# Decode steps of a retention layer moved from TensorE to VectorE and ScalarE

## What is computed

```python
# one step for a sample: chunk length C = 1, per head
S_new = gamma * S + outer(k, v)        # k * k_decay = k, as C - 1 - idx = 0
o     = q @ S_new                      # intra + cross of retention_chunk
```

## Time and profile before

| | |
|---|---|
| median of 3 runs | 1497.14 us |
| profiled execution, first to last instruction | 1495.6 us |
| TensorE clock granted, mean | 0.997 |
| instructions | 28307 |
| bytes moved by DMA | 229.13 MB, mean 153 GB/s |
| VectorE, ScalarE, POOL instructions | 1251, 929, 571 |

### The profile page before, as it was taken

How to read it: one execution, slowest core, us unless ns; L and a number is a source line. 1 busy time by engine, 2 the same in 40 slices (tenths; PEclk the granted TensorE clock), 3 DMA queues, 4 the chain that set the end, 5 groups by cost and what they waited for, 6 DMA issues and landing times.

```text
span 1495.6 us, 28307 instructions
## 1 busy us (share of the span) xinstructions
PE 1475.2 (99%) x11336; PEld 1455.2 (97%) x11336; DVE 1001.0 (67%) x1251; ACT 635.4 (42%) x929; POOL 842.0 (56%) x571
## 2 busy tenths in 40 slices
PE   8999999999999999999999999999999999999996
PEld 5999999999999999999999999999999999999995
DVE  7999888856545724576715876766657765574847
ACT  5533444344544541131213855556556332332333
POOL 3377776777545653257565445555555655554555
PEclk9999999999999999999999999999999999999998
DMA  6013333322356258621421144566759575454634
GB/s 217 22 42 94 114 114 113 113 80 65 112 176 205 75 200 296 219 80 50 149 78 50 29 149 171 199 237 219 253 193 326 203 285 189 142 208 156 227 107 170
DMA packets 110091, 229.13 MB, mean 153 GB/s; under 512 B 8960, under 2 KB 20992, under 8 KB 108304
## 3 DMA queue, kind: packets, MB, share of 16 engines
q1 hardware_dynamic: 95296, 204.30, 39.7%
q10 hardware_dynamic: 14672, 23.09, 4.6%
HBM read 154.41 MB, written 72.95 MB: 152 GB/s over the span
## 4 chain that ended last, share of the span: by engine, by line
PE 96%; POOL 1%; DMA 1%; ACT 1%; issue 1%; DVE 0%; POOLq 0%; SPq 0%; DVEq 0%; ACTq 0%
PE ps L1476 40%; PE ps L1237 26%; PE ps L1026 16%; PE ps L1402 3%; PE ps L1389 3%; PE ps L1074 2%; PE ps L1164 1%; PE ps L1169 1%; PE ps L1180 1%; PE ps L1166 1%; DMA cva_h<-conv_scratch 1%; PE ps L1147 0%; PE ps L1152 0%; PE ps L1194 0%; POOL w_l L931 0%
## 5 line engine op out<-in xcount | busy, mean ns | idle before, releaser
L1476 PE MATMUL ps<-tx_h,w_h 128*128 128x258 f32 x960 | 271.5, 283 | 0.0
L1476 PE MATMUL ps<-tx_l,w_h 128*128 128x258 f32 x960 | 271.3, 283 | 0.0
L1476 PE MATMUL ps<-tx_h,w_l 128*128 128x258 f32 x960 | 271.1, 282 | 0.0
L996 POOL TENSOR_TENSOR w_l<-raw,w_h 128x512 fp32r<-128x512 f32 x120 | 185.6, 1551 | 147.6 <-ACT w_h L2033 147.1
L1476 PE MATMUL ps<-fx_l,w_h 128*128 128x258 f32 x720 | 203.7, 283 | 0.0
L1476 PE MATMUL ps<-fx_h,w_h 128*128 128x258 f32 x720 | 203.6, 283 | 0.0
L1476 PE MATMUL ps<-fx_h,w_l 128*128 128x258 f32 x720 | 203.4, 282 | 0.0
L1476 PEld LDWEIGHTS ps<-tx_h,w_h 128*128 128x128 f32 x960 | 181.4, 189 | 0.1
L1476 PEld LDWEIGHTS ps<-tx_l,w_h 128*128 128x128 f32 x960 | 181.4, 189 | 0.1
L1476 PEld LDWEIGHTS ps<-tx_h,w_l 128*128 128x128 f32 x960 | 181.2, 189 | 0.0
L2328 DVE SCALAR_TENSOR_TENSOR ps<-u_ext,wdw,ps 128x512 f32<-128x512 f32 x232 | 155.2, 749 | 0.0
(11 more groups left out here) (386 smaller groups left out, 4305.4 us busy)
## 6 DMA issues: line engine op xcount, KB each, us to landing
raw<-wseq_dram SPq DMA_DIRECT2D x260, 256.0 KB, 3.1
quad_scratch<-quad_h SPq DMA_DIRECT2D x16, 774.0 KB, 3.5
tx_h<-quad_scratch SPq DMA_DIRECT2D x12, 1032.0 KB, 10.4
tx_l<-hidden_scratch SPq DMA_DIRECT2D x12, 1032.0 KB, 12.8
gate_scratch<-gst SPq DMA_DIRECT2D x10, 1032.0 KB, 5.0
hidden_scratch<-hq_g SPq DMA_DIRECT2D x8, 1032.0 KB, 7.0
hidden_scratch<-stg_b SPq DMA_DIRECT2D x6, 1032.0 KB, 6.9
hq_g<-hidden_scratch SPq DMA_DIRECT2D x6, 1032.0 KB, 13.1
```

Source lines behind the costliest of these rows:

```text
L996: pool.tensor_tensor(lo, src, hi.bitcast(F32), ALU.subtract).then_inc(q_lo, 1)
L1476: out = pe.matmul(ps[:, 2 * n + s, 0:HC], RINGS[q % RING][wa][:, kk * P:(kk + 1) * P], OPS[x][xb][:, QK * kh + kk, at_:at_ + HC], start=(i ...
```

## The change

The state of a sample now lies with the values on partitions: `s_in` and `rets` are laid out by the host as (sample, pair, 128, 512), where the 512 columns are head, half of the values and key dimension. Then o is a sum over columns. VectorE multiplies by broadcast rows of key and query, adds into the decayed state and sums; ScalarE decays the state in place. The rows that are transposed on TensorE and broadcast through memory are keys and queries (2 x 2 x 128) instead of values. `decode_out` and `decode_copy` are gone, and with them their waits. The row buffer `rows_b` is used for the products too, so the next row load waits for `dec_o`, which the last sum raises.

```diff
-DEC_LOAD = {1: 0, 4: 1, 7: 2, 10: 3, 14: 4, 17: 5, 21: 6, 24: 7}
-DEC_STATE = {3: 0, 6: 1, 9: 2, 13: 3, 16: 4, 20: 5, 23: 6, 27: 7}
-DEC_OUT = {4: 0, 9: 1, 11: 2, 14: 3, 18: 4, 21: 5, 25: 6, 30: 7}
-DEC_COPY = {x + 1: n for x, n in DEC_OUT.items()}
+DEC_ROWS = 5
+DEC_LOAD = {7 + 3 * b: b for b in range(DEC)}
+DEC_STATE = {9 + 3 * b: b for b in range(DEC)}
+DEC_STORE = {10 + 3 * b: b for b in range(DEC)}
...
-            def v_decode(p):
-
-                for t in range(4):
-                    out = pe.transpose(ps[0:DEC, 7, t * P:(t + 1) * P], vv[p][:, t, SEQ:T], ident[:])
-                out.then_inc(vs_T, 1)
+            def sample_rows(p):
+
+                for n, t in enumerate((2, 3, 0, 1)):
+                    out = pe.transpose(ps[0:DEC, 7, n * P:(n + 1) * P], qk[p][:, t, SEQ:T], ident[:])
+                out.then_inc(row_T, 1)
...
                 if x in RET_A:
                     if RET_A[x] == 0:
-                        pe.wait_ge(vs_cp, 1)
+                        pe.wait_ge(ln_n, 8)
+                        x_evicted(pe, X_V[0][1], "e5")
+                        x_evicted(pe, X_V[0][1], "e7")
+                        pe.wait_ge(rope_done, 4)
+                    if RET_A[x] == 2:
+                        pe.wait_ge(row_cp, 1)
                     chunk_a(0, RET_A[x])
...
-                if x in DEC_OUT:
-                    n = DEC_OUT[x]
-                    x_evicted(pe, v if j > 1 else v - 1, "e2")
-                    if n:
-                        pe.wait_ge(dec_cp, n)
-                    decode_out(0, n, 2 * decode_bank(x), HC + 2 + 4 * n).then_inc(dec_o, 1)
+                if x == DEC_ROWS:
+                    pe.wait_ge(s_upd, 3)
+                    sample_rows(0)
...
+                last.then_inc(mm, 1)
                 chunk_b(1, c)
-                if c > 1:
-                    last = decode_out(1, c - 2, 3 * (g % 2), CH + 8)
-                last.then_inc(mm, 1)
...
             def decode_load(p, b):
...
+                n = b + DEC * p
+                act.wait_ge(ss_st[b % 2], 16 + 16 * (n // 2))
+                if n > 1:
+                    act.wait_ge(dec_o, n - 1)
+                act.dma_start(s_dec[:, b % 2, :], s_in[b, p]).then_inc(ss_ld[b % 2], 16)
+
+            def row_load(p, b):
+
+                n = b + DEC * p
+                if n:
+                    act.wait_ge(dec_o, n)
+                act.wait_ge(row_st, 16 * p + 16)
+                act.dma_start(rows_b[:], rscr[p, b:b + 1, :].broadcast_to([P, 4 * DK])).then_inc(row_ld, 16)
+
+            def decode_decay(p, b):
+
+                n = b + DEC * p
+                act.wait_ge(ss_ld[b % 2], 16 * (n // 2 + 1))
+                for h in range(2):
+                    s_h = s_dec[:, b % 2, h * DV:(h + 1) * DV]
+                    act.activation(s_h, s_h, ACT.Copy, scale=float(GAMMA[2 * p + h])).then_inc(s_dcy, 1)
...
                 if i == 4:
-                    act.wait_ge(dec_cp, DEC * (p + 1))
+                    act.wait_ge(dec_o, DEC * (p + 1))
...
-                if v == X_GB[3]:
-                    act.wait_ge(s_new, DEC + 1)
...
             for c in range(NRC):
                 chunk_values(1, c)
                 if c > 1:
+                    decode_decay(1, c - 2)
                     decode_store(1, c - 2)
                 if c:
                     decode_load(1, c - 1)
-                    value_load(1, c - 1)
+                    row_load(1, c - 1)
                 chunk_output(1, c)
...
+            decode_decay(1, DEC - 2)
             state_store(1)
             taken(act, G_AOUT + NRC - 1)
             norm_square(1, 0)
             decode_store(1, DEC - 2)
             decode_load(1, DEC - 1)
-            value_load(1, DEC - 1)
+            row_load(1, DEC - 1)
             norm_square(1, 1)
             for i in range(2 * CHUNKS):
                 norm_root(1, i)
                 if i == 0:
+                    decode_decay(1, DEC - 1)
+                if i == 1:
                     decode_store(1, DEC - 1)
...
             def decode_state(p, b):
...
+                n = b + DEC * p
+                s_b = s_dec[:, b % 2, :]
+                dve.wait_ge(s_dcy, 2 * n + 2)
+                dve.wait_ge(row_ld, 16 * n + 16)
+                for t in range(4):
+                    s_t = s_b[:, t * P:(t + 1) * P]
+                    out = dve.scalar_tensor_tensor(s_t, rows_b[:, (t // 2) * DK:(t // 2 + 1) * DK],
+                                                   vv[p][:, t, SEQ + b:SEQ + b + 1], s_t, ALU.mult, ALU.add)
                 out.then_inc(s_new, 1)
...
+                dve.wait_ge(s_new, n + 2)
+                q = rows_b[:, 2 * DK:].rearrange("p (h d) -> p h d", h=2)
+                for e in range(2):
+                    out = dve.tensor_tensor(rows_b[:, 2 * e * DK:2 * (e + 1) * DK].rearrange("p (h d) -> p h d", h=2),
+                                            s_b.rearrange("p (h e d) -> p e h d", h=2, e=2)[:, e], q, ALU.mult)
+                out.then_inc(dec_pr, 1)
+                dve.wait_ge(dec_pr, n + 1)
+                for e in range(2):
+                    out = dve.reduce_sum(vv[p].rearrange("p (h e) n -> p e h n", e=2)[:, e, :, SEQ + b],
+                                         rows_b[:, 2 * e * DK:2 * (e + 1) * DK].rearrange("p (h d) -> p h d", h=2),
+                                         mybir.AxisListType.X)
+                out.then_inc(dec_o, 1)
```

More of the change, by code:

```diff
@@ L342, in build @@
         ss_st = [sem("ss_st0"), sem("ss_st1")]
-        vb_ld = sem("vb_ld")
-        s_kv = sem("s_kv")
+        row_ld = sem("row_ld")
+        s_dcy = sem("s_dcy")
         s_new = sem("s_new")
@@ L1172, in chunk_b @@
                 out.then_inc(ret_b, 1)
[L1174 to L1183, removed]
             def out_stat(p, i):
@@ L1213, in unit_bank @@
                     x_evicted(pe, v - 1, "e2")
-                    read = [n for x, n in DEC_OUT.items() if x <= turn(v, 1)]
-                    if read:
-                        pe.wait_ge(dec_cp, max(read) + 1)
                 elif k == 4:
@@ L1330, in b_part @@
                         between(sub)
-                if g in (G_BO0, G_BO0 + 1):
-                    out = decode_out(1, DEC - 2 + g - G_BO0, 3 * (g % 2), CH + 8)
                 out.then_inc(mm, 1)
@@ L1656, in sig_rows, with sample_rows_out @@
                 act.activation(sgm[:, k:k + n, :] if v in X_G else rows, rows, ACT.Sigmoid).then_inc(xg_sg, 1)
-            def v_decode_out(p):
-                act.wait_ge(vs_T, p + 1)
-                act.activation(v_bc[0:DEC], ps[0:DEC, 7, :], ACT.Copy).then_inc(vs_cp, 1)
-                act.wait_ge(vs_cp, p + 1)
-                act.dma_start(vscr[p], v_bc[0:DEC]).then_inc(vs_st, 16)
+            def sample_rows_out(p):
+                act.wait_ge(row_T, p + 1)
+                act.activation(rows_b[0:DEC], ps[0:DEC, 7, :], ACT.Copy).then_inc(row_cp, 1)
+                act.wait_ge(row_cp, p + 1)
+                act.dma_start(rscr[p], rows_b[0:DEC]).then_inc(row_st, 16)
             def ln_square(j):
@@ L1711, in decode_load @@
             def decode_load(p, b):
-                act.wait_ge(ss_st[b % 2], 16 + 16 * (b // 2 + p * (DEC // 2)))
-                if p == 0 and b > 1:
-                    act.wait_ge(dec_o, b - 1)
-                elif p == 1 and b < 2:
-                    act.wait_ge(dec_o, DEC)
-                elif p == 1:
-                    act.wait_ge(mm, done(S_AOUT + b))
-                act.dma_start(s_dec[:, b % 2, :].rearrange("p (h e) -> p h e", h=2),
-                              s_in[b, 2 * p:2 * p + 2].rearrange("h p e -> p h e")).then_inc(ss_ld[b % 2], 16)
-            def value_load(p, b):
-                act.wait_ge(s_new, b + NRC * p + 1)
-                act.wait_ge(vs_st, 16 * p + 16)
-                act.dma_start(v_bc[:], vscr[p, b:b + 1, :].broadcast_to([P, 2 * DV])).then_inc(vb_ld, 16)
+                n = b + DEC * p
[15 more added lines that the diff above has]
+                    act.activation(s_h, s_h, ACT.Copy, scale=float(GAMMA[2 * p + h])).then_inc(s_dcy, 1)
             def decode_store(p, b):
-                act.wait_ge(s_new, b + NRC * p + 2)
-                act.dma_start(rets[b, 2 * p:2 * p + 2].rearrange("h p e -> p h e"),
-                              s_dec[:, b % 2, :].rearrange("p (h e) -> p h e", h=2)).then_inc(ss_st[b % 2], 16)
+                act.wait_ge(s_new, b + DEC * p + 2)
+                act.dma_start(rets[b, p], s_dec[:, b % 2, :]).then_inc(ss_st[b % 2], 16)
             def state_store(p):
@@ L2491, in decode_state @@
-                dve.wait_ge(s_kv, n * 2 + 2)
-                for h in range(2):
-                    hs = slice(h * DV, (h + 1) * DV)
-                    out = dve.scalar_tensor_tensor(s_dec[:, b % 2, hs], s_dec[:, b % 2, hs], float(GAMMA[2 * p + h]),
-                                                   v_bc[:, hs], ALU.mult, ALU.add)
-                out.then_inc(s_new, 1)
-            def decode_copy(p, b, bank, col):
```

(3 more changed lines are left out.)

66 lines of the change are left out of this document (20 added, 46 removed).

## The result

The changed kernel takes 1499.49 us (median of 20 runs, 1498.21 to 1500.97), the kernel before in the same comparison 1497.38: a ratio of 1.0014, interval 1.0008 to 1.0020. The forecast was 1485.7. The profiled execution has a span of 1497.8 us where the one before had 1495.6.

What follows compares the result with a forecast made beforehand. TensorE, busy 99%, was taken as the bound: -14.4 us of decode matmuls, +1.2 in pair 0, +1.8 in the tail, -11.4 in sum, giving 1485.7 us. The range was 1482.6 to 1490.5, holding some 0.83.

Steps and rivals of the forecast that it cites:

- What leaves TensorE: Decode matmuls in both pairs: 0.90 us per step, 16 steps, 14.4 us removed, all on the path.
- What ScalarE gets: Two decays per step, 0.7 us, 11 us in all; POOL's ring slot freed sooner in pair 1 priced at nothing.
- The new wait: Row load waits for dec_o; in the A_OUT loop a worst row delays a step 2 us, inside over 3 us slack.
- Rival (d): A_OUT loop paced by the single row buffer's round trip, making the kernel slower: 1501.7 us; chance 0.05.
- The ports: VectorE stretched beside POOL's work: one stretch of 1.0 us per step, chance 6 in 8 in pair 0, none in loop.
- six of the eight sets: Pair 0 sets counted as having a VectorE stretch beside POOL before the change; basis for the 6 in 8 odds.
- Pair 0, the tight places: Steps 1, 3, 5 make TensorE wait 0.9, 0.6, 0.1 us if stretched; 1.2 us with odds, bounds 0 and 4.6.
- The tail: End of pair 1: round trip step 6, row, step 7 gives back 1.8 of 2.7 us, bounds 0.9 and 2.9.
- VectorE's undisturbed step: A decode step on VectorE without hold-ups: 2.5 us, one more than before, 16 us over the kernel.

Runs made afterwards that it cites:

- x2: Changed kernel with each decode step's two-input VectorE operations (state update, query product) replaced by reductions of the same widths: 1483.31 us, ratio 0.9902 to the kernel before.
- x16: Changed kernel with semaphore mm rising in chunk_b again in pair 1's A_OUT loop, so GpSimd's split starts later: 1491.44 us, ratio 0.9959 to the kernel before.
- x7: Changed kernel with pair 0's steps at other turns, state loads ahead of stores, and steps of four 512-column VectorE instructions: 1494.90 us, ratio 0.9980 to the kernel before.
- x13: x7 plus GpSimd waiting in the A_OUT loop for the chunk's decode step before splitting the next weight slot: 1488.69 us, ratio 0.9938 to the kernel before.

## Why the prediction was wrong

**What leaves TensorE: right.** The period of a chunk is 9.43 us as forecast (584.75 to 594.18 in the chain of waits), and x2 is 14.2 us below the kernel before, against 14.4.

**What ScalarE gets: the step that failed.** "POOL's ring slot is freed a few us sooner in pair 1 [...]: nothing, since POOL waits for the ring and not PE for it" looked at who waits for POOL, and not at what POOL's work runs beside. The freed slot started the split 3.4 us earlier in the chunk, next to VectorE's new step. x16 puts the semaphore back to where the split begins 5.2 us after chunk_a instead of 3.0: 8.0 us. In the terms of the sum, pair 1 gave back 8.0 us where 1.8 were charged, and pair 0 gave back 8.2 (5.7 of waits and 2.5 of half clock) where 1.2 were. The first is this step, the second the size of the port stretches with what followed from it, below.

**The new wait: half right.** The late row came as forecast (8.50 us, step 4 late by 1.9), inside TensorE's slack. But the slack was read for TensorE alone; 2 us late was enough to fall beside GpSimd, which kept steps 5 and 6 late in their turn. Rival (d), a round trip that paces the loop, is not what happened: the period stayed at 9.43.

**The ports: mis-sized, in the loop from nothing.** Charged were 1.0 us per stretch in pair 0 and none in the loop, because before there was none in the loop. But before, GpSimd stood elsewhere in the chunk. The count of "six of the eight sets" was misread too. Only two of the six stretches lay in the fused operations. The others lay in the copy and in the multiply by a scalar, which have one SBUF input and which the new step does not have, such as these two of the trace of before:

```profile
390.43 1.67 DVE L2489 TENSOR_SCALAR v_bc<-v_bc,qk 128x256 f32<-128x256 f32 x2
...
490.31 1.25 DVE L2484 COPY qd_b<-qk 128x2 f32<-128x2 f32 x1
```

And a block is not held once: each of several operations in a row can be held by a GpSimd instruction of its own. The four of step 4 in pair 0 took 3.98 us where 1.14 is free, and those of step 5 3.83. Of the four of step 4 one took 341 ns and the others 1116 to 1381, beside three GpSimd instructions:

```profile
469.84 3.98 DVE L2470 SCALAR_TENSOR_TENSOR s_dec<-rows_b,v,s_dec 128x128 f32<-128x128 f32 x4 [1.63 <-ACT s_dec L1706]
...
479.83 3.83 DVE L2470 SCALAR_TENSOR_TENSOR s_dec<-rows_b,v,s_dec 128x128 f32<-128x128 f32 x4 [0.31 <-ACT s_dec L1706]
...
469.52 1.29 POOL L930 TENSOR_TENSOR wx_l<-wx_y,wx_h 128x512 fp32r<-128x512 f32 x1
470.95 1.41 POOL L912 TENSOR_TENSOR wx_y<-raw 128x512 f32<-128x512 f32 x1
472.33 1.34 POOL L930 TENSOR_TENSOR w_l<-wx_x,w_h 128x512 fp32r<-128x512 f32 x1
```

The prediction cited the rule of the Trainium skill (SBUF — State Buffer, "Practical consequences" under the port table) that a VectorE instruction with two SBUF inputs contends with a GpSimd one that reads SBUF, and a reduction never. The trace agrees: reductions kept to 409 to 424 ns, both kinds with two inputs reached 1.4 us and more. What failed was my count, of blocks where instructions had to be counted.

**Pair 0, the tight places: the three places right, one size wrong.** For steps 1, 3 and 5 waits of 0.9, 0.6 and 0.1 us were worked out with one stretch each; measured are 0.4, 1.2 and 4.1, at these steps and nowhere else. The sum with its odds was 1.2, the bound 4.6; it is 5.7, and 2.5 us of half clock behind the last. Step 5 had 0.9 us to spare and lost them twice over: its own operations took 2.7 us too long, its products 0.9, and it began late, since the store and then the state load behind step 4's 3.98 us landed only at 479.04. That one step's stretch passes to the next through ScalarE's queue was not in the sum. The stretch sizes in pair 0 were no bound either: "no set before had more than 1.5 us of them". That hold-ups make pair 0's share is read from these rows and from x2, which removes them from every step; no run keeps GpSimd away in pair 0 alone.

**The tail: the charged wait is not there, another one is.** The 1.8 us, with a bound of 2.9, were for the third B_OUT group, which was to wait for product_gate behind step 7 and its row. TensorE has no such wait. The wait for osq at the first out_stat was named too, with 0.9 us at most; it is 5.3, and 2.8 us of half clock. The sum took step 5 as on time and lets only step 6 be stretched; steps 4 and 5 of the loop were held too, and the lag grew over three steps. x16 shows the tail without that. Counted from the end of chunk_b(7), step 6 is over at 5.0 us, where 5.1 was worked out, step 7 at 10.9 instead of 12.1 or more, and the gate product at 12.5; the third group starts at 13.1, and TensorE waits for none of them. So the round trip of the single row buffer cost nothing there.

**Neither sum nor range had the clock.** Two waits, of 4.1 and 5.3 us, cost 2.5 and 2.8 us each on top. No row of before has a long wait of TensorE in these stretches, and I did not look for one elsewhere.

**VectorE's undisturbed step: right.** 1.14 + 0.76 + 0.75 us with gaps, 2.7 against 2.5; reductions 0.41.

## What to carry to other kernels

When an edit moves a semaphore, ask not only who waits for the engine it releases but what that engine's work will now run beside: here a start of its work 2.2 us sooner (3.0 us after chunk_a instead of x16's 5.2), on an engine with 7 us of idle time per chunk, cost 8.0 us. Count each VectorE instruction with two SBUF inputs as open to one GpSimd instruction of its own, and if GpSimd has idle time, let it wait for the step: one wait won back 7.9 us. A slack is to be held against every engine that shares something with the late work, and a wait of TensorE as long as the 4.1 and 5.3 us here is to be priced with the slow stretch behind it.

## What the runs showed of the hardware that I had not expected

- Back-to-back short operations are held one by one: four of 346 ns took 3.98 us beside three GpSimd instructions in a row (469.52 to 473.67), three of the four being held, while no reduction took over 424 ns.
- Behind waits of 4.1 and 5.3 us TensorE's granted clock was 0.50 for 3 to 4 us. A product of 24 matmuls took 5.40 instead of 2.88 us. Idle matmuls in the wait kept it at 1.00 and saved 3.5 us of the run, though VectorE was nearly as late.
- A lag sustained itself: step 4 late, held by GpSimd, so step 5 late, held again. The runs of x7 differ by 11 us, and those of the same kernel with GpSimd kept away (x13) by 1.8. A small spread is no proof of the contrary: the changed kernel's own 20 runs lie within 2.8 us.
